# Experts of a two-layer backbone: the second product with its operands exchanged, and weights in two slots of 512 columns instead of three of 256

## What is computed

```
aff = softmax(xf @ w_router)
gate, idx = top_k(aff.T, 2 * t // 16)
xe = xf[idx]
h = silu(xe @ w_e1) * (xe @ w_e3)
ye = (h @ w_e2) * gate
out = zeros_like(xf).at[idx].add(ye)
```

## Time and profile before

| | |
|---|---|
| median of 3 runs | 4451.14 us (4449.66 to 4455.37) |
| the profiled execution | 4446.32 us, span 4444.3 us, mean granted clock 0.929 |
| PE busy | 3881.5 us (87% of the span) |
| PEld busy | 3009.2 us (68%) |
| DVE, ACT, POOL busy | 2144.0, 975.0, 1061.9 us |
| first product of the experts, L2559, 8192 instructions | 1048.5 us busy |
| second product, L2567, 4096 instructions | 547.2 us busy |
| DMA | 836.17 MB, mean 188 GB/s |

### The profile page before, as it was taken

One profiled execution on the slowest core, in us unless ns is written; L12 is line 12 of the kernel. 1 busy time (PEld: TensorE's weight loads), 2 busy tenths in 40 slices (PEclk: granted clock), 3 DMA queues, 4 the chain that ended last, 5 costly groups with the idle time before them and its releaser, 6 DMA issues. The chain is left out here.

```text
span 4444.3 us, 80407 instructions
## 1 busy us (share of the span) xinstructions
PE 3881.5 (87%) x33680; PEld 3009.2 (68%) x33680; DVE 2144.0 (48%) x4904; ACT 975.0 (22%) x1962; POOL 1061.9 (24%) x1092
## 2 busy tenths in 40 slices
PE   4999967888697999999769998788878699999994
PEld 3444546776456999999744445566654389999994
DVE  3335046656465454544453330556646564445544
ACT  2233134444110000000033321444331100000001
POOL 0036034453220100001040450354522100100003
PEclk9999978888898999999889998888889799999997
DMA  7557353331526888888564752334226368888884
GB/s 269 169 188 249 128 131 77 81 69 34 199 97 212 290 284 281 281 294 289 175 229 152 246 196 70 90 80 94 57 55 219 122 228 291 294 279 282 283 291 172
DMA packets 557877, 836.17 MB, mean 188 GB/s; under 512 B 85864, under 2 KB 403368, under 8 KB 551372
## 3 DMA queue, kind: packets, MB, share of 16 engines
q1 hardware_dynamic: 474476, 720.51, 49.8%
q10 hardware_dynamic: 67840, 71.59, 4.9%
q0 software_dynamic: 15200, 38.94, 3.5%
HBM read 698.83 MB, written 132.10 MB: 187 GB/s over the span
## 5 line engine op out<-in xcount | busy, mean ns | idle before, releaser
L2559 PE MATMUL ffn_hb<-ffn_xT,ffn_w 128*128 128x144 f32 x8192 | 1048.5, 286 | 0.0
L2559 PEld LDWEIGHTS ffn_hb<-ffn_xT,ffn_w 128*128 128x128 f32 x8192 | 1019.6, 190 | 2.3 <-issue 1.0
L521 PE MATMUL front_acc<-front_w,front_xmT 128*128 128x512 f32 (+2 forms) x2304 | 877.3, 540 | 18.2 <-DVE front_xmT L782 18.2
L521 PEld LDWEIGHTS front_acc<-front_w,front_xmT 128*128 128x128 f32 x2304 | 436.4, 192 | 445.1 <-issue 418.4
L2567 PE MATMUL ffn_acc<-ffn_hT,ffn_w 128*128 128x144 f32 x4096 | 547.2, 287 | 0.0
L2567 PEld LDWEIGHTS ffn_acc<-ffn_hT,ffn_w 128*128 128x128 f32 x4096 | 518.5, 190 | 6.7 <-issue 6.7
L2602 ACT ACTIVATE ffn_en<-ffn_hb 128x144 f32<-128x144 f32 x256 | 74.5, 291 | 1446.3 <-PE ffn_hb L2559 1446.3
L2482 POOL DMA_INDIRECT ffn_xe<-scratch_xhat,ffn_g_idx x34 | 34.2, 1007 | 1466.9 <-DVEq L2667 1424.7
L2711 DVE TENSOR_TENSOR ffn_hT<-ffn_en,ffn_hb 128x144 f32<-128x144 f32 x256 | 77.8, 304 | 582.6 <-ACT ffn_en L2602 582.2
L2256 PE MATMUL mixer_acc<-mixer_wout,mixer_oT 128*128 128x512 f32 x576 | 256.2, 603 | 3.2 <-DMA mixer_wout<-in_w_out 1.7
L2628 DVE TENSOR_SCALAR_CACHE_REDUCE ffn_junk<-ffn_row,ffn_pair 128x128 f32<-128x128 f32 (+2 forms) x324 | 245.2, 757 | 1.4
(11 more groups left out here) (334 smaller groups left out, 5141.4 us busy)
## 6 DMA issues: line engine op xcount, KB each, us to landing
ffn_w<-in_w_e SPq DMA_DIRECT2D x384, 1024.0 KB, 9.5
x_res<-in_w_mod SPq DMA_DIRECT2D x40, 1024.0 KB, 5.4
x_res<-scratch_proj SPq DMA_DIRECT2D x36, 768.0 KB, 6.1
scratch_proj<-front_out ACTq DMA_DIRECT2D x90, 256.0 KB, 2.2
ffn_row<-scratch_affT SPq DMA_DIRECT2D x36, 576.0 KB, 4.5
front_w<-in_w_in ACTq DMA_DIRECT2D x8, 2048.0 KB, 12.9
scan_qk<-scratch_qkv SPq DMA_DIRECT2D x16, 1024.0 KB, 10.0
scratch_qkv<-x_res SPq DMA_DIRECT2D x18, 768.0 KB, 3.5
```

Of the source, the lines that this page charges most:

```text
L521: mm = pe.matmul(acc[:, U % 2, 0:size], xmT[:, k, t * P:(t + 1) * P], w[:, n % 2, k, 0:size], start=k == 0, stop=k == KD - 1)
L2559: mm = pe.matmul(hb[:, b, i * CAP:(i + 1) * CAP], w[:, r, k, c:c + P], xT[:, s, k, :], start=k == 0, stop=k == KD - 1)
```

## The change

The second product holds `hT` in the array and moves `w2`: for the sample rows two products of 512 columns with 128 columns of weights, for the prompt rows four products of 256 columns with 32 columns of weights (16 of them prompt rows, 16 zeros), one at each quarter of the array, each on its quarter of the features. The sum then lies row by feature, as `output` needs it: `turn_y`, the copies to `yT` and `yTp`, and their semaphores are gone, and `output(e)` reads `acc` at the end of its own expert instead of early in the next. `down_products(0)` waits for `output` of the expert before, since `acc` is read by it. The prompt part is scattered in pieces of 256 features instead of 128; half of the 128 lines of `yp` are padding, and their indices point to 32 added rows of `moe`, which `mixer_output` also clears. Weights come in two slots of four pieces, so half an expert is loaded at a time, and a row of w1 or w3 gives 2 KB in place of 1 KB.

```diff
+                        sp.dma_start(T["moe"][ROWS:ROWS + 32, :], zeros[0:32]).then_inc(moe_zero, 16)
...
-    RING = 3
-    WIDTH = 2
+    RING = 2
+    WIDTH = 4
     PER = KF // WIDTH
-    PER_BANK = 512 // CAP
...
-        hT = st.sb("hT", [P, 2, CAP])
-        yT, yTp = st.sb("yT", [P, KD, CAP_S]), st.sb("yTp", [P, KD, CAP_P])
-        ye, yp = st.sb("ye", [P, D]), st.sb("yp", [P, P])
+        hT = st.sb("hT", [P, 2, CAP_S + 32])
+        ye, yp = st.sb("ye", [P, D]), st.sb("yp", [P, D // 4])
...
-                    for src, dst, k in ((ye, T["moe"], 0), (yp, pieces("moe"), 1)):
+                    for src, dst, k in ((ye, T["moe"], 0), (yp, pieces("moe", D // 4), 1)):
...
-                def turn_y(e):
-
-                    pe.wait_ge(yT_done, e * 2 + 3)
-                    for k in range(KD):
-                        pe.transpose(tr[:, k * P:(k + 1) * P], yT[:, k, :], B.ident)
-                    pe.transpose(ypT, yTp[:].rearrange("p k n -> p (k n)"), B.ident).then_inc(y_turned, 1)
...
                     def down_products(j):
                         r, b = slot_of(e, j), j % 2
                         pe.wait_ge(h_done, e * KF + j + 2)
-                        for c in range(KD):
-
-                            mm = pe.matmul(part(c), w2[:, r, j % WIDTH, c * P:(c + 1) * P], hT[:, b, :], start=j == 0 and c % PER_BANK == 0,
-                                           stop=j == KF - 1, skip_group_check=True)
+                        if j == 0:
+                            pe.wait_ge(y_done, e + 1)
+                        w = w2[:, r, j % WIDTH, :]
+                        for q in range(4):
+                            pe.matmul(acc[32 * q:32 * q + 32, 2, 0:D // 4], hT[:, b, CAP_S:CAP_S + 32], w[:, q * D // 4:(q + 1) * D // 4], start=j == 0,
+                                      stop=j == KF - 1, skip_group_check=True)
+                        for n in range(2):
+                            mm = pe.matmul(acc[:, n, :], hT[:, b, 0:CAP_S], w[:, n * 512:(n + 1) * 512], start=j == 0, stop=j == KF - 1, skip_group_check=True)
                         if j % WIDTH == WIDTH - 1:
                             mm.then_inc(w_used[r], 1)
...
-                    if not first:
-                        turn_y(e - 1)
...
-                            pe.wait_ge(y_done, e + 1)
                             turn_x(e + 1)
...
-                    act.wait_ge(w_used[slot_of(e, KF - 1)], fills(e, KF - 1) + 2)
-                    for b in (1, 2):
-                        k, y = by_piece(b)
-                        act.activation(yT[:, k, :], y[:, :, 0:CAP_S], ACT.Copy)
-                        ins = act.activation(yTp[:, k, :], y[:, :, CAP_S:], ACT.Copy)
-                    ins.then_inc(yT_done, 1)
...
+                    dve.tensor_scalar(picks[:, e, 4:5], slot_p[:, 0:1], B.quarters, B.quarter, ALU.mult, ALU.add).then_inc(own, step())
...
-                    dve.wait_ge(y_turned, e + 2)
-                    dve.tensor_scalar(ye[:], tr[:], picks[:, e, 1:2], None, ALU.mult).then_inc(own, step())
-                    dve.tensor_scalar(yp[:], ypT, picks[:, e, 3:4], None, ALU.mult).then_inc(own, step())
+                    dve.wait_ge(w_used[slot_of(e, KF - 1)], fills(e, KF - 1) + 2)
+                    dve.tensor_scalar(ye[:], acc[:, 0:2, :].rearrange("p n c -> p (n c)"), picks[:, e, 1:2], None, ALU.mult).then_inc(own, step())
+                    dve.tensor_scalar(yp[:], acc[:, 2, 0:D // 4], picks[:, e, 3:4], None, ALU.mult).then_inc(own, step())
...
-                            if not first:
-
-                                dve.wait_ge(rows_added, e)
-                                index(s_idx, e - 1, None)
-                                output(e - 1)
...
-                    dve.wait_ge(w_used[slot_of(e, KF - 1)], fills(e, KF - 1) + 2)
-                    k, y = by_piece(0)
-                    dve.tensor_copy(yT[:, k, :], y[:, :, 0:CAP_S]).then_inc(own, step())
-                    dve.tensor_copy(yTp[:, k, :], y[:, :, CAP_S:]).then_inc(own, step())
+                    dve.wait_ge(rows_added, e + 1)
+                    index(s_idx, e, 4, None)
+                    output(e)
...
+    ids[:, -3] = p // CAP_P
+    ids[:, -2] = np.where(p % 32 < CAP_P, 4, 0)
+    ids[:, -1] = np.where(p % 32 < CAP_P, p // 32, ROWS * 4 + p)
```

More of the change, by code:

```diff
@@ L2162, in _ @@
                 sp.wait_ge(all_stored, 17)
-                sp.wait_ge(moe_zero, 16 * TILES + 1)
+                sp.wait_ge(moe_zero, 16 * (TILES + 1) + 1)
                 for s in range(2):
@@ L2418, in experts @@
         later = st.sb("later", [P, P])
-        picks = st.sb("picks", [P, E_N + 2, 4])
+        picks = st.sb("picks", [P, E_N + 2, 5])
         acc, hb = st.ps("acc", [P, 3, 512]), st.ps("hb", [P, 2, 512])
         tr, trp = st.ps("tr", [P, D]), st.ps("trp", [P, 512])
-        xpT, ypT = trp[:, 0:P], trp[:, P:2 * P]
+        xpT = trp[:, 0:P]
         found_s, found_p = trp[:, 2 * P:3 * P], trp[0:32, 3 * P:4 * P]
@@ L2426, in experts @@
         w_used = [st.sem(f"w_used{i}") for i in range(RING)]
-        idx_done, turned, xT_done, h_prod, silu_done, h_done, yT_done = (
-            st.sem(x) for x in ("idx_done", "turned", "xT_done", "h_prod", "silu_done", "h_done", "yT_done"))
-        y_turned, y_done, rows_added, passed = (st.sem(x) for x in ("y_turned", "y_done", "rows_added", "passed"))
+        idx_done, turned, xT_done, h_prod, silu_done, h_done = (
+            st.sem(x) for x in ("idx_done", "turned", "xT_done", "h_prod", "silu_done", "h_done"))
+        y_done, rows_added, passed = (st.sem(x) for x in ("y_done", "rows_added", "passed"))
         row_in, ranked, sel_done, summed, copied, picked = (st.sem(x) for x in ("row_in", "ranked", "sel_done", "summed", "copied", "picked"))
@@ L2433, in experts @@
         gathered, scattered = B.gathered, B.scattered
[L2434 to L2440, removed]
+        pieces = lambda name, n: T[name].rearrange("r (k c) -> (r k) c", c=n)
         def slot_of(e, j):
@@ L2479, in gather @@
                 def gather():
-                    for dst, src, k in ((xe, T["xhat"], 0), (xp, pieces("xhat"), 1)):
+                    for dst, src, k in ((xe, T["xhat"], 0), (xp, pieces("xhat", P), 1)):
                         at = bass.IndirectOffsetOnAxis(ap=g_idx[:, k:k + 1].bitcast(U32), axis=0)
@@ L2592, in _ @@
                 turns(pe, body)
-                turn_y(E_N - 1)
             @block.scalar
@@ L2615, in _ @@
                 dve.memset(pair[:], 0.0).then_inc(own, step())
+                dve.memset(hT[:, :, CAP:], 0.0).then_inc(own, step())
                 dve.tensor_tensor(later[:], B.masks[:, 1, :], B.ident, ALU.subtract).then_inc(own, step())
@@ L2658, in rank_picked, with index @@
                     dve.tensor_copy(picks[:, e, 3:4], slot_p[:, 1:2]).then_inc(own, step())
-                def index(idx, e, signal):
+                    dve.tensor_scalar(picks[:, e, 4:5], slot_p[:, 0:1], B.quarters, B.quarter, ALU.mult, ALU.add).then_inc(own, step())
+                def index(idx, e, at, signal):
                     if step.count:
                         dve.wait_ge(own, step.n)
-                    dve.tensor_copy(idx[:], picks[:, e, 0:4:2]).then_inc(own, step())
+                    dve.tensor_copy(idx[:], picks[:, e, 0:at + 1:at]).then_inc(own, step())
                     dve.wait_ge(own, step.n)
@@ L2693, in _ @@
                 rank_picked(0)
-                index(g_idx, 0, idx_done)
+                index(g_idx, 0, 2, idx_done)
                 rank_start(1)
@@ L2738, in body @@
                     step.restart()
-                    dve.sem_inc(yT_done, 1)
                 turns(dve, body)
-                dve.wait_ge(rows_added, E_N)
-                index(s_idx, E_N - 1, None)
-                output(E_N - 1)
 def last_residual(nc, T, B):
@@ L2833, in host_constants @@
     rope = np.ascontiguousarray(rope.reshape(TILES, P, 2, half).transpose(1, 0, 2, 3))
-    ids = np.zeros((P, TILES + P + 2 + CH + 1), np.float32)
+    ids = np.zeros((P, TILES + P + 2 + CH + 3), np.float32)
     ids[:, :TILES] = np.arange(ROWS).reshape(TILES, P).T
@@ L2860, in build @@
         B.rope = sb("rope_sb", [P, TILES, 2, ROPE // 2])
-        B.ids = sb("ids_sb", [P, TILES + P + 2 + CH + 1])
+        B.ids = sb("ids_sb", [P, TILES + P + 2 + CH + 3])
         B.dsel = B.ids[:, TILES + P:TILES + P + 2]
         B.half_mask = B.ids[:, TILES + P + 2:TILES + P + 2 + CH]
-        B.piece = B.ids[:, TILES + P + 2 + CH:]
+        B.piece, B.quarters, B.quarter = (B.ids[:, TILES + P + 2 + CH + i:TILES + P + 3 + CH + i] for i in range(3))
         B.zero = sb("zero", [P, 32])
```

8 lines of the change are left out of this document (4 added, 4 removed).

## The result

The changed kernel takes 4574.69 us (median of 4 runs, 4565.32 to 4576.96) against 4453.26 us (4 runs, 4449.66 to 4455.65): a ratio of 1.0271, with a 95% interval of 1.0254 to 1.0287. It is 121 us slower; the forecast was 4516 us, and its range ended at 4555. The profiled execution took 4576.96 us, its span is 4575.2 us, its mean granted clock 0.929 as before.

The account below looks back on a forecast made before the run. TensorE's stream alone was taken to bound the stage; 84.7 + 2.8 - 29.4 + 11.0 - 3.8 = +65.3 us, 4511.6 us on the profiled execution, forecast as 4516 us, range 4465 to 4555.

Parts of the forecast that it names:

- One piece's down_products: Second product of a mid-expert piece on TensorE: 2.34 us against 1.96, 224 times +0.378, +84.7 us in all.
- second 0.10 of the way out: Extra 0.10 us on the second wide instruction after narrow ones, left out since 512 columns stream longer than any weight load.
- I take nothing: Weight loads on the DMA engines: a half takes 17.0 us, window 23.2 us, so no cost to TensorE.
- 1.3 us that I put around the packets: Fixed time of a weight load beside its packets, from a quarter of 8.6 us landing after 9.9 us.
- at worst 23.1, still just inside: Half load's longest time if gather and scatter interleave with the weights, against a window of 23.2 us.
- q0 held up until the weights have drained: Gather and scatter queue on the DMA engines waits behind queued weights, so it costs the weights nothing.
- two slots are too few: Rival, 12%: loads exceed 23.2 us through interleaving and slow 2 KB packets; 24 us loads give +50 us, 4566 us.
- Beginning: Start of each layer's experts: two halves queued ahead delay the first gather by 5.5 us, +11.0 us in all.
- about +5: Upper bound at each layer's beginning: us more if the clock falls in idle time and spins after turn_x slow.
- End: End of each layer: the last sum is read 2.4 us earlier, less 0.5 us, giving 2 x -1.9 = -3.8 us.
- Narrow products overlap: Eight 32-column-weight instructions on TensorE run four at once in 0.43 us; rival of no overlap, 4846 us, 2%.
- Faster, since the loads are the bound: Rival, 5%: TensorE is bound by weight loads, not columns, so fewer loads give -147 us, 4304 us.

Follow-up runs that it names:

- e3: The changed kernel with GpSimd waiting until the second half's weights have landed before it issues gather and scatter: 4546.87 us, ratio 1.0220.
- e1: The kernel before with two slots of 512 columns and nothing else of the change: 4493.67 us, ratio 1.0098.
- e8: e1 with gather and scatter issued only after the second half's weights have landed: 4458.05 us, ratio 1.0015.
- e6: The changed kernel, a layer's first expert getting its second half of weights issued only after the first gather has landed: 4571.01 us, ratio 1.0270.
- e2: The changed kernel with three slots of 256 columns as before, so only the exchange of operands is left: 4533.65 us, ratio 1.0203.
- e4: e2 with the narrow products of two pieces made together after every second piece, hT in four buffers: 4492.52 us, ratio 1.0103.
- e7: The changed kernel with narrow products of four pieces together, late gather and scatter, and the first expert's second half after the first gather: 4476.82 us, ratio 1.0057.
- e9: e8 with the second half of a layer's first expert issued only after the first gather has landed: 4450.19 us, ratio 0.9990.

## Why the prediction was wrong

The direction, the mechanism of the largest term and most prices were right, the size was not: +65.3 us forecast, +121 measured, +125 in the stretches. Step by step:

- **One piece's down_products: 2.34 us forecast, 2.48 measured.** Two terms failed. The prediction left out the "second 0.10 of the way out", with the argument that a 512-column stream is longer than any weight load; it is there nevertheless: the second wide instruction starts 0.53 us after the first (1838.59), the next ones 0.43 apart. And beside the two rounds stand 0.14 us, not 0.10. The step was to grow by 7 x 0.378 + 0.09 - 0.98 = 1.76 us and grew by 2.87: seven times 0.14 and 0.1 in the eighth piece. 32 x 1.11 = 36 us too little. The row for it was there: the earlier trace rows show the second 0.10 behind `sum_picks`. What causes it is open; the length of the stream does not take it away, as I had argued.
- **Weights, "I take nothing": +27 us.** A half load takes 19.6 us alone (e3) where I had 17.0, at worst 18.5. The 1.3 us that I put around the packets are mis-sized: e3's row is slow at both ends, 0 to 211 GB/s in its first slices and 23 to 47 in its last. The gather and scatter add 4.8 (forecast, if they interleave, 4.6). The prediction's "at worst 23.1, still just inside" became 24.4 us against a window of 23.4, forecast 23.2. TensorE waiting for ffn_w at piece 4 was one of its signs of being wrong. A second step that failed is the reading of 6.9 against 4.5 us as "q0 held up until the weights have drained". The gather is late because its first packet is: in the kernel before it comes 4.4 us after the issue in mid-stage and 1.9 at a layer's first gather. After that q0's packets go among the weights and cost them their time. The rule of the Trainium skill (DMA: Bandwidth & Descriptors, "SWDGE vs HWDGE vs iDMA") that an engine takes turns between the two kinds of queue, which I weighed and didn't take, agrees with the trace after, 101 packets of q0 and 100 of q1 in the same 2 us, and 19.9% of the engines for q0 during the load. What I derived from it, that the first gather would then wait for nothing, does not: that gather landed after 7.9 us in place of 4.5. The rival "two slots are too few" (12%) came half true: its mechanism is interleaving, as it said, but packets of 2 KB move at some 390 GB/s, above the 349 it asked for, and the wait is paid 30 times and not 62. It falls at piece 4 alone; the load for piece 0 of the next expert, which meets no gather, takes 19.6 us (issued at 1800.09).
- **It was the place of gather and scatter and not the number of slots.** e1 and e8 differ by one wait on GpSimd and by 34 us.
- **Beginning: +11.0 forecast, 2 x 6.4 = +12.8 measured, for partly other reasons.** That the two are near is luck. The gather landed 7.9 us after its issue, 3.4 later than before, and not 5.5 (10 us after issue); 2.9 us are the lower clock of turn_x and spins, which stood in the bounds as "about +5". The later start also hides a wait of `sum_picks` for VectorE of 1.1 us a layer that the kernel before has too (2.3 us over both layers) and that e6 brings back: 2 x 5.3 = +10.6 net.
- **turn_y -0.98 us, its copies free, no wait of down_products(0) for `output`:** right. Piece 0 to piece 1 takes 4.02 us in e2 and after, in place of 5.00.
- **End: -1.9 us a layer forecast.** Right. ye starts 2.4 us earlier, as forecast. From there to the landing of the last scatter it takes 9.6 and 9.3 us in the two layers, in place of 9.1 and 9.2: 0.1 to 0.5 us more, where 0.5 was forecast.
- **Narrow products overlap, 512 columns at 0.429 us, the clock in the experts 1.00:** right. "Faster, since the loads are the bound" is refuted by e2, which has a quarter fewer loads in the second product and is slower. PEld's busy share fell from 68% to 59% while the time rose.

Added up: 65.3 forecast, + 36 changes of shape, + 27 late weights (30 x 0.91), and the beginnings as forecast = 128 us; the stretches have 125, the medians 121. So the error is the changes of shape, 36 us, and the weights, 27; the rest of the sum together is right to a few us.

## What to carry to other kernels

Where a product is bound by its moving columns, exchanging operands pays by columns: here 4 x 512 = 2,048 for the sample rows against 16 x 144 = 2,304 for all, and a thin remainder of 16 rows that needs its own shape eats it up. In columns alone an expert now takes 8 x (1.71 + 0.43) = 17.1 us, where the old way with turn_y took 8 x 1.96 + 0.98 = 16.7; with the changes of shape it is 16.7 + 2.87 = 19.5. Before splitting off a remainder, count how many times the stream changes between narrow and full weights, at 0.33 us each, and do the narrow products in batches (e4, e7).

When loads are bunched, count everything else that the DMA engines do in the window of one load, at its full share, and then look at who decides when it starts: one wait that put gather and scatter behind the load was worth 27 to 34 us here. And a DMA that lands later under load is no sign that it was held until the others drained: look at when its first packet moves and at what both queues do from then on.

## What I had not expected of the hardware

- A change from full-width to 32-column weights and back costs 0.33 us in a float32 stream even with 512-column products behind it: 0.09 going in, 0.14 coming out, 0.10 on the first wide instruction. Behind 8, 16 or 32 narrow instructions it is the same.
- A gather that is issued while weights are moving lands after 7.0 to 8.1 us (after), with no weights moving after 4.0 to 4.4 (e9). The difference is not in the sharing but ahead of it: the first packet comes after 4.3 to 4.6 us in place of 1.6 to 1.9.
- Behind 6 us of spins at 1.00 TensorE stood idle for 3.4 us, and turn_x then ran at 0.50.
